# Moving 640 bytes of small tables ahead of the large buffers in SBUF, in a diffusion layer on one core

## The reference, cut to what matters

```python
x = x + 0.5 * m_x[2] * swiglu(modulate(rmsnorm(x, norm_g[l, 0]), m_x[0], m_x[1]), ffn1_w1[l], ffn1_w2[l])
ctx = ctx + 0.5 * m_c[2] * swiglu(modulate(rmsnorm(ctx, ...), m_c[0], m_c[1]), ffn1_w1[l], ffn1_w2[l])
px = modulate(rmsnorm(x, norm_g[l, 1]), m_x[3], m_x[4]) @ w_in[l]      # 1024 x 3072
...                                    # retention heads and chunk GMLP groups
x = x + m_x[5] * (jnp.concatenate([ret_x, gm_x], axis=-1) @ w_out[l])
x = x + 0.5 * m_x[8] * swiglu(modulate(rmsnorm(x, norm_g[l, 2]), m_x[6], m_x[7]), ffn2_w1[l], ffn2_w2[l])
return rmsnorm(x, final_g)
```

## The kernel before, in words

| buffers | first byte | modulo 512 |
|---|---|---|
| the 76 KB block | 192 | 192 |
| HH, and what lies over it | 78016 | 192 |
| HL, and what lies over it | 110784 | 192 |
| WR | 143552 | 192 |
| WH | 159936 | 192 |
| WL | 176320 | 192 |
| X | 196224 | 128 |

## Time and profile before

### The profile page before, as it was taken

One profiled execution on the slowest core, in us unless ns is written; L12 is line 12 of the kernel. 1 busy time (PEld: TensorE's weight loads), 2 busy tenths in 40 slices (PEclk: granted clock), 3 DMA queues, 4 the chain that ended last, 5 costly groups with the idle time before them and its releaser, 6 DMA issues.

```text
span 2037.5 us, 26082 instructions
## 1 busy us (share of the span) xinstructions
PE 2000.4 (98%) x10112; PEld 1694.4 (83%) x10112; DVE 1247.5 (61%) x1887; ACT 758.9 (37%) x1098; POOL 511.3 (25%) x371
## 2 busy tenths in 40 slices
PE   7999999999999999999999999999999999999997
PEld 4999988888888888888989898877788888888886
DVE  5987766565788677776353324458556555555555
ACT  4433533333333345455121221445333333334342
POOL 1000033324212102124223232665333421220001
PEclk9999999999999999989999999999999999999998
DMA  8864426656556787732101011121656644466664
GB/s 326 342 269 152 156 78 222 203 198 231 206 191 212 255 295 244 257 103 102 42 21 42 32 42 63 62 83 58 209 193 217 212 160 156 162 216 193 192 194 155
DMA packets 108763, 343.53 MB, mean 169 GB/s; under 512 B 11488, under 2 KB 20960, under 8 KB 90464
## 3 DMA queue, kind: packets, MB, share of 16 engines
q1 hardware_dynamic: 108640, 341.85, 49.1%
HBM read 267.36 MB, written 74.45 MB: 168 GB/s over the span
## 4 chain that ended last, share of the span: by engine, by line
PE 90%; DVE 4%; ACT 2%; issue 1%; DMA 1%; POOL 0%; DVEq 0%; POOLq 0%; SPq 0%; ACTq 0%
PE PS L2150 12%; PE PS L2152 12%; PE PS L2151 12%; PE PS L1992 8%; PE PS L1993 8%; PE PS L1994 8%; PE PS L2192 7%; PE PS L2194 7%; PE PS L2193 7%; PE PS L2108 4%; DVE WVL L1583 1%; PE PS L2368 1%; PE PS L2049 1%; DMA WR<-w_units 1%; PE PS L2029 0%
## 5 line engine op out<-in xcount | busy, mean ns | idle before, releaser
L2150 PE MATMUL PS<-HH,WVH 128*128 128x512 f32 x672 | 262.5, 391 | 0.0
L2152 PE MATMUL PS<-HH,WVL 128*128 128x512 f32 x672 | 261.6, 389 | 0.0
L2151 PE MATMUL PS<-HL,WVH 128*128 128x512 f32 x672 | 261.5, 389 | 0.0
L1992 PE MATMUL PS<-HH,WH 128*128 128x512 f32 x416 | 164.9, 396 | 3.8 <-DVE WL L1774 3.8
L1994 PE MATMUL PS<-HH,WL 128*128 128x512 f32 x416 | 162.0, 389 | 0.0
L1993 PE MATMUL PS<-HL,WH 128*128 128x512 f32 x416 | 161.9, 389 | 0.0
L748 POOL TENSOR_TENSOR WL<-WR,WH 128x512 fp32r<-128x512 f32 x80 | 108.5, 1384 | 210.4 <-ACT WH L927 159.5
L1583 DVE TENSOR_TENSOR WVL<-WR,WVH 128x512 fp32r<-128x512 f32 x160 | 115.3, 721 | 69.2 <-ACT WVH L1010 67.7
L2152 PEld LDWEIGHTS PS<-HH,WVL 128*128 128x128 f32 x672 | 126.1, 188 | 26.6
L2150 PEld LDWEIGHTS PS<-HH,WVH 128*128 128x128 f32 x672 | 126.2, 188 | 26.3 <-ACT U L1042 0.5
L2151 PEld LDWEIGHTS PS<-HL,WVH 128*128 128x128 f32 x672 | 126.2, 188 | 26.0
(11 more groups left out here) (282 smaller groups left out, 4825.2 us busy)
## 6 DMA issues: line engine op xcount, KB each, us to landing
WR<-w_units SPq DMA_DIRECT2D x89, 1024.0 KB, 5.8
gated<-HB SPq DMA_DIRECT2D x44, 512.0 KB, 6.7
down_weight_sums<-WB SPq DMA_DIRECT2D x22, 1024.0 KB, 3.8
gated_sums<-TBF SPq DMA_DIRECT2D x22, 768.0 KB, 4.2
AW<-ada_units SPq DMA_DIRECT2D x12, 1024.0 KB, 13.2
HLF<-down_weight_sums SPq DMA_DIRECT2D x46, 256.0 KB, 3.5
W2RB<-w_units SPq DMA_DIRECT2D x22, 512.0 KB, 3.6
WB<-w_units SPq DMA_DIRECT2D x22, 512.0 KB, 3.6
```

The source lines that it names most:

```text
L1992: pe.matmul(dst, wh, xh, start=first, stop=False)
L2150: pe.matmul(bank[:, :], wh, xh, start=first, stop=False, skip_group_check=True)
L2151: pe.matmul(bank[:, :], wh, xl, start=False, stop=False, skip_group_check=True)
L2152: ins = pe.matmul(bank[:, :], wl, xh, start=False, stop=k == 3, skip_group_check=True)
```

## The change

No instruction is added, removed or put in another place in any engine's list, and no shape changes. Three of the small tables, 640 bytes in all, stand in other places: Z (256 bytes), an 8 x 8 table of scalars for each partition, comes ahead of HH, and GAIN and GATE (192 bytes each), the modulation's coefficients, come between HL and WR.

```diff
+        Z = keep("Z", [P, 8, Z_END], F32)
         HIGHS = top[0]
         HH = keep("HH", [P, KT, SEQ], F32R)
         LOWS = top[0]
         HL = keep("HL", [P, KT, SEQ], F32R)
+        GAIN = keep("GAIN", [P, 3, KT, 2], F32)
+        GATE = keep("GATE", [P, 3, KT, 2], F32)
         W = top[0]
         WR = keep("WR", [P, 2, KT, UC], F32)
         WH = keep("WH", [P, 2, KT, UC], F32R)
         WL = keep("WL", [P, 2, KT, UC], F32R)
         MODS = keep("MODS", [P, NMOD * KT, 2], F32)
         BA = keep("BA", [P, NMOD * KT, 2], F32)
-        GAIN = keep("GAIN", [P, 3, KT, 2], F32)
-        GATE = keep("GATE", [P, 3, KT, 2], F32)
         NG = keep("NG", [P, 3, KT], F32)
...
         IDX = keep("IDX", [P, Z_END], F32)
-        Z = keep("Z", [P, 8, Z_END], F32)
         X = keep("X", [P, KT, SEQ], F32)
```

## The result

| | median | runs | |
|---|---|---|---|
| before | 2034.76 us | 2032.5 to 2035.86, 8 runs | |
| after | 2040.81 us | 2039.34 to 2045.36, 8 runs | ratio 1.0034, 95% interval 1.0026 to 1.0043 |

The change makes the kernel 6.05 us slower, 0.34%. The forecast was no change, 2034.4 us. The 2040.81 us lie just inside its range of 2028 to 2041 us, but not for the reason that the forecast gave.

A forecast was written before the change was run, and what follows sets the result against it. PE's pace per matmul (226.7 ns at 512 columns) times the count of matmuls was taken as the kernel's time. PE, DVE and ACT, DMAs and clock summed to 0, so the forecast was the median, 2034.4 us, range 2028 to 2041 us.

The forecast's parts named there:

- the new distances cost more: Rival on PE: changed tile distances slow matmuls, up to 13.3 ns x 5088 = 67.7 us, 2102 us; chance 0.08.
- the first, PE: First part, 5088 matmuls whose two tiles get another distance: same pace as now, 0 us.
- a tenth of it, 2041.2 us: The slower-distances rival on PE at a tenth of its full price of 67.7 us.
- The collision that goes away: Rival on PE: the matmuls' surplus is two reads colliding and goes; up to 52.9 us less, 1981.5 us; chance 0.15.
- DVE and ACT: Second part, vector and activation work with X at another start: at most 1.0 us to either side, taken as 0.
- The loads into WR: Third part, two DMA loads on the feed-forward chain: -1.7 to +4.8 us for both, taken as 0.
- The clock: Fourth part, half-clock stretch after PE's 1.91 us wait: 1.4 us lost, which could go or come again.

The follow-up runs named there:

- m2: Layer left out, groups of 32 float32r matmuls alone, starts alternating or weights narrower; at 512 columns 228.3 ns alternating together, 229.8 with 64-column weights at distance 0.
- m1: Layer left out, groups of 32 matmuls alone, each at one distance between tile starts; float32r, 512 columns: 226.8 to 227.4 ns at 0, 233.5 at 128.
- e1: Kernel before with only Z moved ahead of HH; 2032.76 us against 2034.89, ratio 0.9995.
- e5: Changed kernel with the 128 bytes of MS also put between HL and WR; 2034.35 us against 2034.04 of before, ratio 0.9996.
- m4: Layer left out, groups of 48 float32r matmuls of 256 columns, most behind 16 plain float32 ones; at starts 192, 192, 0 either about 113.5 or 117.8 ns.
- x2: Kernel before with HCHB and HCLB 192 bytes further inside the 76 KB block, W2RB, PR and SG 256; 2031.35 us against 2034.04, ratio 0.9984.
- x1: Kernel before with HCHB, HCLB, W2RB, PR and SG 192 bytes further inside the 76 KB block; 2032.38 us against 2033.75, ratio 0.9990.
- e3: Kernel before with all three tables, Z, GAIN and GATE, moved ahead of HH; 2046.14 us, ratio 1.0060.
- e4: Kernel before with GAIN and GATE moved ahead of HH and the 128 bytes of MS between HL and WR; 2052.01 us, ratio 1.0086.

## Why the prediction was wrong

The forecast was no change; the rival "the new distances cost more" happened, to which I had given 0.08.

*The part that failed* is the first, PE, taken at 0. Its argument was that L2150 shows 391 ns with HH and with V3H, "the same instruction at another distance between its operands". But that is another distance only in whole kilobytes (28 KB from WVH to HH and 48 KB from V3H to WVH, not the 20 KB that I wrote); modulo 256 both are 0. I had written that all pairs of the trace are alike modulo 512 and still let the one row decide. A quantity that has one value throughout a trace says nothing of its effect, and the constancy of the surplus was a constancy at one single distance.

*The size.* Worked out from the table: 1248 x 5.65 = +7.05 us for HH with WH, 1056 x 0.75 = -0.8 for HCHB, 768 x 0.3 and 192 x 0.9 (HCH) = -0.4 for the mixer's. The sum is +5.8 us, against 6.05 measured. The rival's price had 13.3 ns for all 5088 pairs. In truth 2016 of them, HH with WVH, went to a distance of 256, which is none, 1248 lost 5.65 ns, and the 256-column pairs gained a little. My "a tenth of it, 2041.2 us" fits by luck, by its number and not by its reason.

*The collision that goes away* was right in that a distance can take time out of the surplus: 6.3 ns of 13 at 256 columns and 192 bytes. At 512 columns none of the distances tried does so. That the surplus is a collision is not shown. Of its arguments two stand: at half clock there is no surplus, and plain float32 and bfloat16 have 2.5 ns at the distances tried. The third, that 4-column weights showed 115 ns for 120, bears on 256 columns alone: there m2 has 113.3 ns with 64-column weights for 119.6 with 128, but at 512 columns narrower weights were slower.

*DVE and ACT* were right, 684 to 685 ns and 632 to 633. *The loads into WR* too: 5.8 us, and 6.22 us for the one on the chain. (HLF with 8.2 us was not the slowest group of 1 MB loads, as I had it: the page has AW at 13.2. The loads did not change, so nothing hangs on it.) *The clock* was right as a source of scatter: a profiled execution 4.5 us off its kernel's median made two spans equal that belong to kernels 6 us apart.

The section "Wait — 56ns, not 53.3ns?" of "TensorE: Matmul & The Clock Gate", in the Trainium skill, has 215.7 ns for 512 columns; the bfloat16 groups here agree (215.8), float32r never got there. "Who interferes with whom" in "SBUF — State Buffer", of the Trainium skill too, has separate read ports for the moving operand and the weights and PE waiting on nobody. That no other engine is needed agrees with m1; but where the two tiles start changes PE's pace by up to 7.5 ns of 226.8, with PE alone at work.

*What stays open.* That the pace depends on the two starts modulo 256 is shown by e1 to e5 and m1: at 512 columns with full weights a distance of 128 was at least 4.4 ns slower than 0 in every kernel; at 256 columns one distance can have two paces (m4, x2). Why is not shown. That a weight load and a moving read meet in SBUF was only argued. For it speaks that the cost of 128 bytes is gone with weights of 64 columns (m2); a surplus that does not shrink with them, and a pace that depends on what ran before (m4), fit no simple count of meetings. Several steady paces lie whole steps of 6.7 ns over the columns' time, 120.0 and 113.3 over 106.7, and 226.7 over 213.3, which looks as if the two reads fall into step with one another; no run shows that step itself.

## What to carry to other kernels

In a kernel bound by float32r matmuls of 512 columns, start every moving and every weight tile at the same place modulo 256 bytes; a stray table of 128 bytes between two large buffers costs 2.5% of each matmul that takes one tile from either side of it. For 256 columns no such rule came out: the best pace of a distance may not be the one that a kernel gets (x1, x2). Padding put between buffers is a change to the innermost loop, so count the matmuls of each pair of buffers and their distance before moving anything. And where all rows of a trace share one value of a parameter, they bound nothing about another value: a kernel of some groups of 32 matmuls, under 400 us, gives the whole table of 512 columns in one run.

## What was not expected of the hardware

- Float32r, 512 columns, 128-column weights: 226.8 to 228.0 ns at distance 0, 229.0 at 64, 230.9 to 234.3 at the others tried, with period 256 bytes. Differences of 16 bytes matter (231.8 at 16).
- The best distance tried depends on the width: 0 at 512 columns (226.8), 64 at 448 (200.1 against 202.7) and at 384 (173.3 against 174.3), 192 at 256 (113.3 against 119.6). With weights of 64 columns at 256 it is 0 again (113.3 against 119.0).
- Matmuls on the same starts have more than one pace: in m4 the same 48 of 256 columns, behind the same 16 plain float32 matmuls, took 113.5 ns each the first time and 117.8 the second. In e3 and e4 the products on V2H to V4L slowed from 226.8 to 228.0 ns with their own distance unchanged.
- Plain float32 and bfloat16 took 215.8 ns at each distance tried (0, 64 and 128).
- With weights of 64 columns the cost of a distance of 128 at 512 columns is gone (229.8 ns at 0, 229.2 at 128).
